# Three of four weight sums of a pair move from VectorE to adding DMAs on GpSimd's queue

## What is computed

```python
def first_block(x, mem, ...):                  # cut to its products
    proj = rmsnorm(x, norm_mix_g) @ w_in       # 2048 x 6144
    x = x + mixed @ w_o
    xq, xk, xv = hx @ w_xq, hm @ w_xk, hm @ w_xv
    x = x + xo @ w_xo
    x = x + (silu(hf @ w_gate) * (hf @ w_up)) @ w_down
def hybrid_layer(x, c, ...):
    mod = silu(c) @ w_ada + b_ada              # one row by 2048 x 6144
    proj = h @ w_in
    g = sigmoid(h @ w_merge + b_merge)
    merged = g_a * (y_a @ w_br_attn) + g_p * (y_p @ w_br_pool)
    return x + gate * rmsnorm(merged @ w_out, post_g)
```

## Time and profile before

| | |
|---|---|
| median of 3 runs | 2067.81 us |
| the profiled execution's span | 2065.9 us |
| TensorE (PE) busy | 2054.4 us, 99% |
| VectorE (DVE) busy | 1667.2 us, 81% |
| ScalarE (ACT) busy | 1181.2 us, 57% |
| GpSimd (POOL) busy | 50.0 us, 2% |
| DMA, moved | 453.74 MB, 220 GB/s |

### The profile page before, as it was taken

The page is one execution under the profiler, slowest core; times in us unless marked ns, Lnnn a source line. Parts: engine busy times, 40 slices in busy tenths (PEclk is TensorE's granted clock), DMA queues, the critical chain, the costliest instruction groups (busy, mean ns, idle before and its releaser), DMA issues.

```text
span 2065.9 us, 25348 instructions
## 1 busy us (share of the span) xinstructions
PE 2054.4 (99%) x9334; PEld 1699.8 (82%) x9334; DVE 1667.2 (81%) x1830; ACT 1181.2 (57%) x1533; POOL 50.0 (2%) x84
## 2 busy tenths in 40 slices
PE   9999999999999999999999999999999999999998
PEld 8888888888888888888888888888788888888787
DVE  6877778867766788989889898898777778988875
ACT  7666557656655565555555555555756655654453
POOL 1000000000000000000000000000000000000000
PEclk9999999999999999999999999999999999999999
DMA  9555557655544458777777777776465567789763
GB/s 347 180 172 184 184 180 259 225 182 184 189 158 153 159 185 300 267 259 242 243 237 259 261 242 243 236 270 213 158 214 178 180 201 234 269 285 329 219 197 109
DMA packets 219259, 453.74 MB, mean 220 GB/s; under 512 B 14449, under 2 KB 17153, under 8 KB 219009
## 3 DMA queue, kind: packets, MB, share of 16 engines
q1 hardware_dynamic: 213232, 432.07, 62.9%
q0 software_dynamic: 5616, 19.94, 3.0%
q10 hardware_dynamic: 288, 0.13, 0.0%
HBM read 447.88 MB, written 4.19 MB: 219 GB/s over the span
## 4 chain that ended last, share of the span: by engine, by line
PE 95%; DVE 2%; ACT 1%; issue 1%; DMA 1%; POOL 0%; SPq 0%; DVEq 0%; POOLq 0%; ACTq 0%
PE ps L1117 30%; PE ps L1119 30%; PE ps L1118 29%; PE ps L687 2%; DVE wlo L2494 1%; PE ps L837 1%; PE ps L817 1%; PE ps L921 0%; DMA FR<-in_post_norm_g_dram 0%; PE ps L952 0%; PE ps L963 0%; PE ps L901 0%; DMA FR<-in_x_t_dram 0%; ACT whi L1718 0%; DVE raw L2507 0%
## 5 line engine op out<-in xcount | busy, mean ns | idle before, releaser
L2494 DVE TENSOR_TENSOR wlo<-raw,whi 128x1024 fp32r<-128x1024 f32 x835 | 1010.4, 1222 | 262.8 <-ACT whi L1718 257.4
L1718 ACT ACTIVATE whi<-raw 128x1024 fp32r<-128x1024 f32 x835 | 876.6, 1058 | 564.5 <-PE ps L1119 518.2
L1117 PE MATMUL ps<-whi,bh 128*128 128x512 f32 x1384 | 547.3, 395 | 2.3 <-DVE wlo L2494 2.1
L1119 PE MATMUL ps<-whi,bl 128*128 128x512 f32 x1384 | 539.9, 390 | 0.0
L1118 PE MATMUL ps<-wlo,bh 128*128 128x512 f32 x1384 | 539.2, 390 | 0.0
L1117 PE MATMUL ps<-whi,ah 128*128 128x512 f32 x1080 | 429.3, 398 | 0.2 <-DVE wlo L2494 0.2
L1119 PE MATMUL ps<-whi,al 128*128 128x512 f32 x1080 | 421.6, 390 | 0.0
L1118 PE MATMUL ps<-wlo,ah 128*128 128x512 f32 x1080 | 420.9, 390 | 0.0
L1117 PEld LDWEIGHTS ps<-whi,bh 128*128 128x128 f32 x1384 | 260.1, 188 | 57.0 <-DVE wlo L2494 3.1
L1119 PEld LDWEIGHTS ps<-whi,bl 128*128 128x128 f32 x1384 | 259.8, 188 | 54.7
L1118 PEld LDWEIGHTS ps<-wlo,bh 128*128 128x128 f32 x1384 | 260.2, 188 | 52.5 <-issue 0.2
(11 more groups left out here) (264 smaller groups left out, 1334.6 us busy)
## 6 DMA issues: line engine op xcount, KB each, us to landing
raw<-in_w_in_dram SPq DMA_DIRECT2D x168, 512.0 KB, 4.5
raw<-in_w_ada_dram SPq DMA_DIRECT2D x96, 512.0 KB, 4.6
raw<-in_w_gate_dram SPq DMA_DIRECT2D x88, 512.0 KB, 4.9
raw<-in_w_up_dram SPq DMA_DIRECT2D x88, 512.0 KB, 5.4
raw<-in_w_down_dram SPq DMA_DIRECT2D x88, 512.0 KB, 5.4
raw<-in_w_merge_dram SPq DMA_DIRECT2D x64, 512.0 KB, 5.0
raw<-in_w_o_dram SPq DMA_DIRECT2D x32, 512.0 KB, 4.8
raw<-in_w_xk_dram SPq DMA_DIRECT2D x32, 512.0 KB, 4.7
```

What stands on the lines that cost most here:

```text
L1117: e.matmul(o, xh[:, k, tokens], wh, start=first, stop=False, skip_group_check=more)
L1119: ins = e.matmul(o, xl[:, k, tokens], wh, start=False, skip_group_check=more, stop=kk == 1 and (st.end or st.form in READ))
L1718: done(e.activation(split_at(n)[0], place(item), ACT.Copy), "hi")
L2494: done(e.tensor_tensor(lo, place(stream.entries[n].item), hi.bitcast(F32), ALU.subtract), "lo")
```

## The change

The sums for M5, M6 and M4 become DMAs from SBUF to SBUF with an adding destination, 128 partitions by 4 KB each, issued by GpSimd: 120 of the 160 sums. The difference for M7 stays on VectorE. Each form has a semaphore of its own. The M5 sum is placed six entries ahead of its product instead of two (three instead of one behind the staggered panel), which also moves the loads of b12 and b11 ahead. In GpSimd's written order `add_weights(n)` issues all sums whose place in the stream is at or ahead of entry n; it waits as written below. A load of SyncE that follows an item in its slot waits for every sum that reads that item.

```diff
-        early = 1 if self.panels[f - 1].stagger == "first" else 2
+        early = 3 if self.panels[f - 1].stagger == "first" else 6
         for form, n in (("M5", at["M5"] - early), ("M6", at["M3"] + 1), ("M7", at["M1"] + 2),
                         ("M4", max(at["M2"], at["M6"]) + 1)):
             self.sums_before[n] = at[form]
@@ scalar_program, make
-                        e.wait_ge(s["t_sum"], nth)
+                        e.wait_ge(*sum_done(form, nth))
@@ vector_program
-                    if n in stream.sums_before:
+                    if n in stream.sums_before and stream.entries[stream.sums_before[n]].form == "M7":
                         sum_weights(stream.sums_before[n])
...
+                item, add, _, nth = stream.entries[n]
+                e.wait_ge(*sum_done("M6", nth))
+                e.wait_ge(s["lo"], stream.pairs[nth - 1][1]["M1"] + 1)
+                done(e.tensor_tensor(place(item), place(add), place(item), ALU.subtract), "sum_m7")
@@ pool_program
+            def add_weights(n):
+                while summed[0] <= n:
+                    m, summed[0] = stream.sums_before.get(summed[0]), summed[0] + 1
+                    if m is None or stream.entries[m].form == "M7":
+                        continue
+                    item, add, form, nth = stream.entries[m]
+                    made = stream.pairs[nth - 1][1]
+                    if form == "M5":
+                        e.wait_ge(*loaded(add))
+                        e.wait_ge(*loaded(item))
+                    elif form == "M6":
+                        e.wait_ge(*sum_done("M5", nth))
+                        e.wait_ge(s["lo"], made["M3"] + 1)
+                    else:
+                        e.wait_ge(*sum_done("M6", nth))
+                        e.wait_ge(s["lo"], made["M2"] + 1)
+                    e.dma_start(place(item), place(add), accum_op=ALU.add).then_inc(sum_done(form, nth)[0], 16)
...
+            add_weights(entry_of("kv", 0, 7))
             e.wait_ge(s["half"], stream.end[index["kv", 0]])
             e.wait_ge(s["rel"], 16)
             load_bias(0)
+            add_weights(entry_of("q", 1, 6))
...
             for i in range(2, 8):
+                add_weights(entry_of("m", i - 2, 7))
                 e.wait_ge(*side_taken(index["m", i - 2], 1 - i % 2))
                 if i % 2:
                     e.wait_ge(*ev(index["m", i - 2], 1))
                 load_merge_bias(i)
@@ sync_program, wait_taken
-                    if i in stream.last_sum_of:
-                        e.wait_ge(s["t_sum"], stream.last_sum_of[i])
+                    for form, nth in stream.sums_of.get(i, ()):
+                        e.wait_ge(*sum_done(form, nth))
```

More of the change, by code:

```diff
@@ L242, in __init__ @@
         self.end, self.bset, self.nth, self.role, self.pairs = {}, {}, {}, {}, []
-        self._done, self._set, self.sums = 0, 1, 0
+        self._done, self._set = 0, 1
         self.aside_at, self.ahead = {}, {}
@@ L266, in __init__ @@
             if entry.add is not None:
-                self.last_sum_of[entry.add] = entry.nth
+                self.sums_of.setdefault(entry.add, []).append((entry.form, entry.nth))
         self._places()
@@ L280, in _add_ada, with _entry @@
             self.items.append(("ada", *todo.pop(0)))
[L282 to L285, removed]
+    def _entry(self, item, add=None, form=None, nth=0):
+        self.entries.append(Entry(item, add, form, nth))
         return len(self.entries) - 1
@@ L324, in normal, with product @@
             self._step(n, p, c, hf, tiles=(0, 1), end=(c == chunks - 1 and hf == 1), **more)
-        def product(form, place, add=None, minus=False, **more):
-            at[form] = n = self._entry(place, add, minus)
+        def product(form, place, add=None, **more):
+            at[form] = n = self._entry(place, add, form, q + 1)
             panel, tile, _, half, _ = PRODUCTS[form]
@@ L344, in _pair @@
             normal(f, *next(todo), snap=("v", q))
-        product("M7", b11, b22, minus=True)
+        product("M7", b11, b22)
         normal(f, *next(todo), snap=("s3", q))
@@ L1710, in make @@
                             jobs.start(pause(3))
-                    item, add, _, nth = stream.entries[n]
+                    item, add, form, nth = stream.entries[n]
                     if add is not None:
-                        e.wait_ge(s["t_sum"], nth)
+                        e.wait_ge(*sum_done(form, nth))
                     else:
@@ L2574, in load_gain, with entry_of @@
                             .partition_broadcast(P)).then_inc(s[f"gain{j % 2}"], 16)
+            summed = [0]
+            def add_weights(n):
[15 more added lines that the diff above has]
+                    e.dma_start(place(item), place(add), accum_op=ALU.add).then_inc(sum_done(form, nth)[0], 16)
+            def entry_of(kind, i, h):
+                return stream.last_of_item[stream.items.index(("w", index[kind, i], h // 2, h % 2))]
             e.wait_ge(s["raw7"], 16)
@@ L2585, in pool_program @@
             e.dma_start(tbl[0:32, :], a["rel_bias_table_2"]).then_inc(s["tbl"], 16)
+            add_weights(entry_of("tq", 1, 7))
             root_of("x")
             e.dma_start(CB, a["c_bias"]).then_inc(s["attn_bias"], 16)
-            for name in ("d0", "d1", "d2", "d3"):
+            for name, at_entry in (("d0", ("tq", 2, 7)), ("d1", ("tq", 3, 6)), ("d2", ("tq", 4, 5)), ("d3", ("tq", 5, 5))):
+                add_weights(entry_of(*at_entry))
                 root_of(name)
@@ L2592, in pool_program @@
             e.dma_start(CB, a["c_dec"]).then_inc(s["decay"], 16)
-            for name in ("e0", "e1", "e2", "e3"):
-                root_of(name)
+            for pair, at_entry in ((("e0", "e1"), ("v", 3, 5)), (("e2", "e3"), ("o", 0, 5))):
+                add_weights(entry_of(*at_entry))
+                for name in pair:
+                    root_of(name)
+            add_weights(entry_of("o", 1, 5))
             e.wait_ge(T[1].full, T[1].n("mix3"))
@@ L2601, in pool_program @@
                 e.dma_start(MT[j], mem_v[:, :, j * PW:(j + 1) * PW]).then_inc(s[f"mt{j}"], 16)
+            add_weights(entry_of("xk", 0, 4))
             for j in range(2, 4):
@@ L2604, in pool_program @@
                 e.dma_start(MT[j - 2], mem_v[:, :, j * PW:(j + 1) * PW]).then_inc(s[f"mt{j - 2}"], 16)
+            add_weights(entry_of("xk", 0, 5))
             root_of("r2")
+            add_weights(entry_of("xk", 1, 3))
             root_of("mem")
+            add_weights(entry_of("g", 0, 5))
             root_of("r3")
+            add_weights(entry_of("u", 0, 5))
             e.wait_ge(s["half"], stream.end[index["g", 0]])
@@ L2610, in pool_program @@
             e.dma_start(OH, a["c_oh"]).then_inc(s["onehot"], 16)
+            add_weights(entry_of("g", 1, 2))
             e.wait_ge(A[0].free, A[0].n("rel"))
@@ L2635, in pool_program @@
                 load_merge_bias(i)
+            add_weights(entry_of("m", 7, 7))
             e.wait_ge(*ev(index["m", 7], 1))
@@ L2648, in pool_program @@
                     load_gain(j)
+            add_weights(stream.total - 1)
             for t in range(2):
```

11 lines of the change are left out of this document (8 added, 3 removed).

## The result

The changed kernel takes 2111.6 us (median of 4 runs, 2109.9 to 2118.2), the kernel before 2067.9: a ratio of 1.0216, 95% interval 1.0203 to 1.0228. That is 43.7 us slower. The forecast was 2081.5, 13.6 us slower: right in sign, but less than a third of the loss. The time lies inside the range of 2067 to 2115 only because that range took in half of the rival "crowded"; the forecast's own case ended at 2095.

A forecast was written before the change was run, and what follows sets the result against it. TensorE was taken as the bound, busy 2054.4 of 2065.9 us. Span 2065.9 + 9.7 (merge pairs) + 5.0 (q pair) - 1.0 (relief) = 2079.6, plus 1.9 to the median: 2081.5 us; range 2067 to 2115.

The forecast's parts named there:

- crowded: Rival: adding DMAs fill the engines, sums and weights land late in 19 pairs; about 2125 us, from 2100 up; chance 0.25.
- the forecast's own case: The forecast's main outcome around 2081.5 us, spanning 2073 to 2095 us; chance 0.49.
- VectorE's relief: Taking 120 sums off VectorE shortens TensorE's waits for low parts; credited 1 us, bounds 0 and 2.3.
- the rival that gave it some 6 us: Rival: TensorE's small delays hang on VectorE, up to half of 11.5 us comes back; 2062 us; chance 0.04.
- The adding DMA: Cost of one sum as a DMA: 5.5 us to landing in an ordinary place, 3.3 us of the engines.
- The doubling: Assumption that reading the destination too doubles a sum's engine time, from 1.6 to 3.3 us; landing 1.6 us later.
- sums land early: Rival: sums land in 3.5 to 4.5 us, so exposed places lose 0 to 4 us; 2067 to 2071; chance 0.22.
- M6 in merge pairs: Three merge pairs: M6's sum queues behind GpSimd's wait and bias load; products 3.0, 3.3, 3.4 us late, 9.7 in all.
- The first q pair: First "q" and "ga" panels: M6's sum behind eight bias loads, 5.0 us late; bounds 2 (if it overtakes them) and 6.
- Ordinary pairs: Thirty-six pairs where M6 is the critical sum and M5 and M4 have more room; put at zero loss.
- Crowding: Sums add 19 points to engine shares of 0.79 and 0.84; SyncE's slot waits end some 4 us later; put at zero.

The follow-up runs named there:

- e16: Changed kernel with M5's sums on VectorE two entries ahead, and M6's DMA issued before the bias loads and GpSimd's merge-pair wait: 2068.05 us, ratio 1.0001.
- e5: e2 plus 42 adding DMAs of the same size in feed-forward pairs that nobody needs: 2073.5 us, ratio 1.0027.
- e2: Changed kernel with all sums on VectorE, M5 still placed six entries ahead: 2072.3 us, ratio 1.0022.
- e3: Changed kernel with the 120 DMAs copying instead of adding, so three forms' sums are left out: 2076.6 us, ratio 1.0043.
- e10: Changed kernel with M6's sums back on VectorE, M5 and M4 still adding DMAs: 2097.0 us, ratio 1.0145.
- e8: Changed kernel with only M6's sums as adding DMAs, M5 and M4 on VectorE, M5 six ahead: 2086.2 us, ratio 1.009.
- e15: e10 with M4's DMA a plain copy (its sum left out) while M5 adds: 2074.5 us, ratio 1.003.

## Why the prediction was right or wrong

**VectorE's relief, -1 us: no sign of it.** e16 takes 89 us off VectorE and is 0.1 us from before, with an interval of 2 us to either side; so the rival that gave it some 6 us is refuted, and a credit of 1 us can't be told from nothing. The argument (VectorE runs ahead, only 2.3 us of TensorE's waits name it) holds.

**The adding DMA: right.** Forecast 5.5 us to landing and 3.3 us of the engines, measured 5.0 and 2.8. The doubling, the step I trusted least, holds: 2.8 to 1.4 against a plain copy. By the fit of the Trainium skill ("DMA: Bandwidth & Descriptors", Anatomy of one DMA) the landing would be 3.2 us, an estimate; the plain copy's 3.3 agrees with that number, the adding one's 5.0 doesn't. (The prediction says that by this number its third rival would hold; it is the second, "sums land early".)

**M6 in merge pairs, 9.7 us: mechanism right, size 7.0.** The rows that answer to the earlier trace rows, of after:
```profile
1790.79 0.57 POOL L2566 DMA_DIRECT2D FR<-in_b_merge_dram  x1 [18.43 <-DVE FR L2300]
1791.34 0.89 POOL L2592 DMA_DIRECT2D raw<-raw  x1
...
1797.10 1.06 ACT L1720 ACTIVATE whi<-raw 128x1024 fp32r<-128x1024 f32 x1 [4.84 <-DMA raw<-raw]
1800.05 0.57 ACT L1223 ACTIVATE side<-ps 128x512 f32<-128x512 f32 x1
1800.77 0.47 PE L1119 MATMUL ps<-whi,fbh 128*128 128x512 f32 x1 [1.99 <-ACT side L1223]
```
GpSimd wakes, issues the bias load, then the sum; ScalarE starts M6's high part 5.76 us after the sum's issue (forecast 6.1), and TensorE starts M6 3.7 us after that (forecast 3.95). TensorE waits 2.0 us where I said 3.0; the three places lost 2.1, 2.4 and 2.4 against 3.0, 3.3 and 3.4, by the start of its entries.

**The first q pair, 5.0 us: 2.9.** (By the prediction's own times it is 5.2, 1517.0 less 1511.79.) The sum was issued at 1537.89 and landed after 5.0 us, not 7.6. It did not overtake the bias loads: the last of them landed at 1540.57, the sum at 1542.9. But the last two landed after 2.7 and 3.2 us here and not after 5.7. In before, weight loads took 30.5% of the engines from 1501 to 1507 us; in after there are none in the like stretch, 1533 to 1539. So 2.9 lies within the bounds of 2 and 6 by luck, not by the condition given for the lower one.

**Ordinary pairs at zero: this is the step that failed.** It reads: "both have more room than M6 ... Thirty-six pairs are of this kind, and I put them at zero". I had asked of each sum whether it is ready for its own product, and it is (M5's lands 15.5 us ahead, M4's 8.6). I hadn't asked who else hangs on it. Two things were in the diff and in the text ahead of the prediction: the placement moves the loads of b12 and b11 forward, and so all others behind them back; and SyncE's one queue stands for M4's landing. The second stood under "Crowding", with the right size for a single stop ("some 4 us later", 5.6 to 9.4 measured), and I put it at zero. The third, M5's sum amid the loads that follow the stop, stood there only as engines that are full everywhere. In place of zero, feed-forward lost 26.3 us (16 pairs) and the start 4.6.

**The rival "crowded loads", 2125:** right where it said that the loss would lie and that loads which follow a sum in their slot are late; half right in its cause. Full engines alone don't do it: e5 has them at 0.9 us more than e2 in feed-forward. Behind a stop they do count, as the place above shows. Its price, 2 us a pair in 19 pairs, would have been near (1.6 in the 16 of feed-forward). It deserved more than its quarter, above all for the slots.

**"Sums land early":** refuted, the landing is 5.0. In e3, where it is 3.3, the merge places lose 2.1 us in all and the first q pair 2.4, together 4.5, a little over that case's 0 to 4.

The sum as it should have stood for the profiled run: start 4.6, attention 1.0, feed-forward 26.3, M6's places 2.9 + 7.0, and 8.4 for other late loads of the last stage and what the clock takes there (below): 50.2 us.

## What to carry to other kernels

When an operation is made slower but "still in time", follow its completion to everyone who waits for it, the in-order load queue first: what is late next is not its own consumer but a load behind it. A cover is one account: the placement took 4.3 of 10.7 us, M4's stop or M5's DMA alone another 1.3 or 1.1, each nearly without harm; both together reached the floor of about 3 us, and from there all is paid. Measure what is left (landing to use) before adding a second cost. Work given to a helper engine must not stand in its queue behind waits that have nothing to do with it: three lines that moved M6's sum ahead of such waits were worth 13.7 us.

## What the runs showed of the hardware

**A wait of TensorE can cost more than it lasts.** Behind the wait at the first q pair, timeline and window (busy, granted clock, DMA share, GB/s) of after:
```profile
1546.06 0.60 PE L1119 MATMUL ps<-whi,fbh 128*128 128x512 f32 x1 [2.74 <-ACT side L1223]
1546.45 0.63 PE L1120 MATMUL ps<-wlo,fbh 128*128 128x512 f32 x1
...
1549.44 0.50 PE L1121 MATMUL ps<-whi,bl 128*128 128x512 f32 x1
1549.78 0.39 PE L1119 MATMUL ps<-whi,bh 128*128 128x512 f32 x1
...
1545.00:1550.00 5.00, 3.94 (x10) 0.66 1.03 336
```
Eight matmuls start 0.43 us apart where the others start 0.23 apart: the clock is at 1.2 instead of 2.4 GHz for 3.4 us, and the 2.74 us wait is followed by another 8 x 0.2 = 1.6 us. The trace of after has six such stretches (at 805.7, 850.0, 1116.2, 1546.1, 1802.2 and 1894.4), 47 slow matmuls, 9.4 of the 50.2 us (4.6 in feed-forward, 4.8 later); its mean granted clock is 0.994, before's 0.999. The waits in front of them last 1.8 to 2.8 us. Before has no such stretch between its first product and its last. Not every wait does it: behind the 2.2 us wait that ends at 1847.9 there is none, nor behind e10's of 2.8 us (804.3) and e8's of 3.0 us (1521.9). So the same lateness costs different sums in different runs, which fits the scatter: after's four runs take 2109.9, 2110.9, 2112.4 and 2118.2 us at mean granted clocks of 0.997, 0.998, 0.997 and 0.994, and e10's 2090.9, 2095.4, 2098.6 and 2100.5 us at 0.999, 0.998, 0.998 and 0.996. Before's four lie from 2067.5 to 2070.6. That the clock makes the scatter wasn't tested; it also means that the profiled run of after, with 50.2 us, holds more clock loss than the median's 43.7.

**An adding DMA from SBUF to SBUF** of 512 KB: 5.0 us to landing and 2.8 us of all 16 engines, against 3.3 and 1.4 for a copy; its issue takes GpSimd 0.86 us against 0.55 (the M4 copies of e15). The Trainium skill ("DMA: Bandwidth & Descriptors", Rules for kernel authors) says that such a DMA reads its destination and writes it later; twice the engine time agrees.
